# Five gather places instead of three, 336 dense tokens instead of 342, and a gate table in eight stages

## What is computed

```python
        q = (xb @ w_query).reshape(TOKEN_BLOCK, PEER_HEADS, 2, PEER_QDIM // 2)
        s = jnp.einsum("nhpd,hpkd->nhpk", q, sub_keys).astype(jnp.float32)
        sv, si = lax.top_k(s, PEER_TOPK)
        ...
        g = jax.nn.softmax(top_s, axis=-1).reshape(TOKEN_BLOCK, PEER_HEADS * PEER_TOPK)
        u = u_tab[eidx]
        hid = jax.nn.gelu(jnp.einsum("nd,ned->ne", xb, u), approximate=False)
        w = (g * hid.astype(jnp.float32)).astype(xb.dtype)
        return jnp.einsum("ne,ned->nd", w, v_tab[eidx])
```

## Time and profile before

| | |
|---|---|
| median of three runs | 3299.02 us (3294.02 to 3302.07) |
| the profiled execution's own time | 3297.2 us |
| its span, first to last instruction | 3295.1 us |
| TensorE busy | 3225.9 us (98%) |
| VectorE busy | 2697.7 us (82%) |
| ScalarE, GpSimd busy | 1053.1 us (32%), 1154.9 us (35%) |
| DMA, mean over the span | 278 GB/s, 914.55 MB |
| gathers | 171 of u, 171 of v |

### The profile page before, as it was taken

One profiled execution on the slowest core, in us unless ns is written; L12 is line 12 of the kernel. 1 busy time (PEld: TensorE's weight loads), 2 busy tenths in 40 slices (PEclk: granted clock), 3 DMA queues, 4 the chain that ended last, 5 costly groups with the idle time before them and its releaser, 6 DMA issues. The chain is left out here.

```text
span 3295.1 us, 48421 instructions
## 1 busy us (share of the span) xinstructions
PE 3225.9 (98%) x19393; PEld 2975.4 (90%) x19393; DVE 2697.7 (82%) x3810; ACT 1053.1 (32%) x1401; POOL 1154.9 (35%) x602
## 2 busy tenths in 40 slices
PE   6999999998999999999999999999999999999998
PEld 3788888888995448999999999999999999999998
DVE  2599999998885669968788888888688888888888
ACT  3223232323222004952323322323322323323332
POOL 2343333332541765013233333334133333233332
PEclk9999999999999999999999999999999999999999
DMA  9745454445557112569899999999799998999887
GB/s 400 282 165 172 157 175 161 167 169 214 196 184 288 64 39 98 226 261 362 337 371 359 355 358 362 353 346 367 291 360 356 357 351 346 361 351 353 341 341 306
DMA packets 174476, 914.55 MB, mean 278 GB/s; under 512 B 16303, under 2 KB 54104, under 8 KB 80088
## 3 DMA queue, kind: packets, MB, share of 16 engines
q1 hardware_dynamic: 125046, 553.37, 45.5%
q0 software_dynamic: 49248, 358.63, 28.0%
HBM read 876.31 MB, written 34.55 MB: 276 GB/s over the span
## 5 line engine op out<-in xcount | busy, mean ns | idle before, releaser
L1441 ACT ACTIVATE sb_raw_hi<-sb_raw_ring 128x2048 fp32r<-128x2048 f32 x256 | 491.0, 1918 | 1144.5 <-DMA sb_raw_ring<-in_v_t 561.3
L1962 DVE TENSOR_TENSOR sb_raw_lo<-sb_raw_ring,sb_raw_hi 128x2048 fp32r<-128x2048 f32 x256 | 585.0, 2285 | 107.1 <-ACT sb_raw_hi L1441 107.0
L1102 PE MATMUL ps_all<-sb_w_hi,sb_raw_hi 128*128 128x342 f32 x2032 | 639.5, 319 | 7.5 <-ACT sb_raw_hi L1441 3.9
L1041 PE MATMUL ps_all<-sb_h_hi,sb_raw_hi 128*128 128x342 f32 x2048 | 646.0, 320 | 0.0
L1041 PE MATMUL ps_all<-sb_h_lo,sb_raw_hi 128*128 128x342 f32 x2048 | 645.6, 320 | 0.0
L1103 PE MATMUL ps_all<-sb_w_lo,sb_raw_hi 128*128 128x342 f32 x2032 | 638.6, 320 | 0.0
L2291 POOL DMA_INDIRECT sb_gather_ring<-in_u_tab,sb_kept x171 | 293.3, 1715 | 747.4 <-DVE sb_kept L2092 571.0
L2291 POOL DMA_INDIRECT sb_gather_ring<-in_v_tab,sb_kept x171 | 298.7, 1747 | 625.6 <-DVE sb_acc_a L2105 425.4
L2195 POOL TENSOR_TENSOR sb_w_low<-sb_w_raw,sb_w_high 128x1536 fp32r<-128x1536 f32 (+1 forms) x63 | 260.0, 4127 | 406.8 <-ACT sb_w_high L1250 406.8
L1102 PEld LDWEIGHTS ps_all<-sb_w_hi,sb_raw_hi 128*128 128x128 f32 x2032 | 384.7, 189 | 10.0 <-ACT sb_raw_hi L1441 5.6
L1041 PEld LDWEIGHTS ps_all<-sb_h_lo,sb_raw_hi 128*128 128x128 f32 x2048 | 386.0, 188 | 0.0
(11 more groups left out here) (311 smaller groups left out, 5367.5 us busy)
## 6 DMA issues: line engine op xcount, KB each, us to landing
sb_raw_ring<-in_u_t SPq DMA_DIRECT2D x128, 1024.0 KB, 7.3
sb_raw_ring<-in_v_t SPq DMA_DIRECT2D x128, 1024.0 KB, 7.7
sb_arena<-in_ada_wt SPq DMA_DIRECT2D x96, 512.0 KB, 4.3
sb_w_raw<-in_w_t SPq DMA_DIRECT2D x32, 1024.0 KB, 5.8
...
```

What stands on the lines that cost most here:

```text
L1041: last = mm(acc, raw_hi[:, r[0], kk * P:(kk + 1) * P], part[:, kk, :], start=i == 0, stop=False)
L1102: mm(accs[c], v, w_hi[:, slots[e], :], start=e == 0, stop=False)
L1441: acti(raw_hi[:, k % 2, :], raw_ring[:, k % RAW, :], ACT.Copy).then_inc(S["un_hi"], 1)
L1962: vec.tensor_tensor(raw_lo[:, k % RAW, :], raw_ring[:, k % RAW, :], raw_hi[:, k % 2, :].bitcast(f32), ALU.subtract)\
```

## The change

XT goes from 42 to 48, so that ND = 336; the last tile's sparse tokens stand twice in the partitions (XG = 2, 96 of 128 rows used) and need 64 slots instead of 43. DOTS is 192, and there are 384 gathers instead of 342, spread over the same steps. The gate table has eight stages of 42 tokens. The ring has five places: while dots are taken, `acc_a` and `acc_x` (not yet accumulators) are places 3 and 4, and while v is accumulated, the two operands of the dots, `h2a` and `h2x`, are. `gather_places` gives each gather the allowed place that was used longest ago, and with it the gather whose use must be over; the first ten and the last six use three places only. The first two gathers into the new places also wait for `w_lo`, since the early units' results lie there. The load of the first two `last_x` tiles, which goes to `h2a` and `h2x`, moves from unit 137 to unit 251. To free two semaphores, `rows_in`, `dist_in` and `silu_in` become one, `head_in`, waited for at its full count by all.

```diff
-XT = 42
+XT = 48
...
+WIDE = 5
...
-STAGE = 38
+STAGE = 42
...
+def gather_places():
+
+    places, last = [], [-1] * WIDE
+    for n in range(2 * DOTS):
+        if n == DOTS:
+            last[GRING:] = [DOTS - 1] * (WIDE - GRING)
+        allowed = range(WIDE if 10 <= n < 2 * DOTS - 6 else GRING)
+        place = min(allowed, key=lambda p: last[p])
+        places.append((place, last[place]))
+        last[place] = n
+    return places
+
+
+GPLACES = gather_places()
+
+
+def gather_use(n):
+    return sum(p == GPLACES[n][0] for p, _ in GPLACES[:n + 1])
...
 def slot_at(n):
-    m, j = n // 4, n % 4
-    return (False, SLOTS + m) if j == 1 else (True, 3 * m + max(j - 1, 0))
+    m, j = n // 3, n % 3
+    return (False, SLOTS + m) if j == 1 else (True, 2 * m + j // 2)
...
-        stage = [placed(f"stage{n}", a, [P, NKEYS, STAGE]) for n, a in enumerate((M0, at))]
+        stage = [placed(f"stage{n}", a, [P, NKEYS, STAGE]) for n, a in enumerate((M0, at) if NSTAGE % 2 else (at, M0))]
...
+        def gather_at(n):
+            place = GPLACES[n][0]
+            if place < GRING:
+                return gather_ring[:, place, :]
+            return ((acc_a, acc_x) if n < DOTS else (h2a, h2x))[place - GRING]
...
-            sp.wait_ge(S["silu_in"], 32)
+            sp.wait_ge(S["head_in"], 96)
...
-                if k == TURN + 3:
-
-                    sp.wait_ge(S["gr_used"], DOTS)
+                if k == UNITS - 5:
+
+                    sp.wait_ge(S["gr_used"], 2 * DOTS - 6)
                     for t in range(2):
                         sp.dma_start(last_x[t], x1_d[t * P:(t + 1) * P, :]).then_inc(S["last_in"], 16)
...
-            dve.wait_ge(S["rows_in"], 48)
+            dve.wait_ge(S["head_in"], 96)
             e, z, q = lg_t
...
-                wait(dve, f"gr_in{n % GRING}", 16 * (n // GRING + 1))
-                ring = gather_ring[rows, n % GRING, :]
+                wait(dve, f"gr_in{GPLACES[n][0]}", 16 * gather_use(n))
+                ring = gather_at(n)[rows, :]
...
-                wait(pool, "gr_used", n - GRING + 1)
-                pool.indirect_dma_start(out=gather_ring[:, n % GRING, :], out_offset=None, in_=u_tab if n < DOTS else v_tab,
+                wait(pool, "gr_used", GPLACES[n][1] + 1)
+                if n < DOTS and GPLACES[n] in ((GRING, -1), (GRING + 1, -1)):
+                    pool.wait_ge(S["w_lo"], EARLY)
+                pool.indirect_dma_start(out=gather_at(n), out_offset=None, in_=u_tab if n < DOTS else v_tab,
```

More of the change, by code:

```diff
@@ L269, in build_program @@
         hid_all = take(DOTS)
+        at = max(at, SM + 2 * PEER_HEADS * NKEYS)
         raw_hi = rounded("raw_hi", at, [P, 2, D])
@@ L351, in bank @@
             return psum[:, i * NB:(i + 1) * NB]
-        names = """consts rows_in dist_in x_in sumsq silu_e silu colsT cols_ev lg_e
-            silu_rows silu_out silu_in col_in0 col_in1 col_in2 col_in3 col_a col_used late_cols late_t late_row late_out bias_in silu_w gate2_cols gate2_t gate2_bias gate2_row gate2_out
+        names = """consts head_in x_in sumsq silu_e silu colsT cols_ev lg_e
+            silu_rows silu_out col_in0 col_in1 col_in2 col_in3 col_a col_used late_cols late_t late_row late_out bias_in silu_w gate2_cols gate2_t gate2_bias gate2_row gate2_out
             ada_in0 ada_in1 ada_in2 ada_in3 ada_in4 ada_done ada_ev row_t mod_b xtr h_tmp h_high h_low
@@ L361, in build_program @@
             x1_out h2x_in xe_in un_in0 un_in1 un_in2 un_hi un_lo un_half un_done g_in0 g_in1 gelu gated w_hi w_lo y_ev
-            gr_in0 gr_in1 gr_in2 gr_used hid_gelu hid_w fin_in last_in last_rest y_last pick_x yt_done sq_done zs y y_out
+            gr_in0 gr_in1 gr_in2 gr_in3 gr_in4 gr_used hid_gelu hid_w fin_in last_in last_rest y_last pick_x yt_done sq_done zs y y_out
             dve pool spare""".split()
@@ L481, in _ @@
             piece_load(0, 3)
-            sp.dma_start(lg_all, decay.partition_broadcast(P)).then_inc(S["rows_in"], 16)
-            sp.dma_start(lam_in, lams.partition_broadcast(P)).then_inc(S["rows_in"], 16)
-            sp.dma_start(iota[:, :], iota_c).then_inc(S["rows_in"], 16)
+            sp.dma_start(lg_all, decay.partition_broadcast(P)).then_inc(S["head_in"], 16)
+            sp.dma_start(lam_in, lams.partition_broadcast(P)).then_inc(S["head_in"], 16)
+            sp.dma_start(iota[:, :], iota_c).then_inc(S["head_in"], 16)
             sp.wait_ge(S["silu_out"], 16)
             sp.wait_ge(S["ada_done"], ADA_PIECES)
-            sp.dma_start(dist, dist_c).then_inc(S["dist_in"], 16)
+            sp.dma_start(dist, dist_c).then_inc(S["head_in"], 16)
             for g in range(GROUPS):
@@ L497, in _ @@
             for g in range(GROUPS):
-                sp.dma_start(silu_b[:, g, :], silu_d[g:g + 1, :].partition_broadcast(P)).then_inc(S["silu_in"], 16)
-            sp.wait_ge(S["silu_in"], 32)
+                sp.dma_start(silu_b[:, g, :], silu_d[g:g + 1, :].partition_broadcast(P)).then_inc(S["head_in"], 16)
+            sp.wait_ge(S["head_in"], 96)
             head_loads(0, first=True)
@@ L1817, in plain @@
                 link(ins)
-            dve.wait_ge(S["dist_in"], 16)
+            dve.wait_ge(S["head_in"], 96)
             head_step(0, None, plain)
@@ L2097, in accumulate @@
                 rows = slice(0, P if own else XP)
-                wait(dve, f"gr_in{n % GRING}", 16 * (n // GRING + 1))
-                ring, acc = gather_ring[rows, n % GRING, :], (acc_a if own else acc_x)[rows, :]
+                wait(dve, f"gr_in{GPLACES[n][0]}", 16 * gather_use(n))
+                ring, acc = gather_at(n)[rows, :], (acc_a if own else acc_x)[rows, :]
                 if n - DOTS in (0, 1):
@@ L2263, in _ @@
                 x1_root(t)
-            pool.wait_ge(S["rows_in"], 48)
+            pool.wait_ge(S["head_in"], 96)
             for hd in range(PEER_HEADS):
```

2 lines of the change are left out of this document (1 added, 1 removed).

## The result

The changed kernel takes 3340.12 us (median of five runs, 3317.94 to 3348.89) against 3299.02 for the kernel before (3294.02 to 3304.53): a ratio of 1.0117, 95% interval 1.0077 to 1.0156. It is slower by some 39 us; the forecast was 3288 and the range ended at 3325. The profiled execution of the changed kernel took 3317.94 us and is the fastest of its five, so its trace shows only about half of the loss; the times of the other four lie 20 to 31 us above it.

A forecast was written before the change was run, and what follows sets the result against it. TensorE was taken to bound the expert loop, with DMA and VectorE close behind. Terms -28.8 - 2.3 + 11 + 6 + 3 = -11.1 us on 3297.2 gave 3286.1, forecast as a 3288 us median; range 3270 to 3325.

The forecast's parts named there:

- columns: Dense expert loop, units 16 to 255: 6 fewer columns at 0.41 ns each shorten every matmul; -28.8 us with two early units.
- gate table: Routing stage: 88 groups instead of 90, with narrower products on VectorE and TensorE; -2.3 us.
- before unit 25: First gathers into the new places wait for w_lo, so dots 10 and 11 run late and TensorE stops; +11 us.
- body: table loads, VectorE: Expert loop: more gathers make table loads land later, +6 us; VectorE at 90% stays below TensorE, 0.
- tail: Last units: residual tiles moved to unit 251, unit 255's load and VectorE's added accumulation, 1 us each; +3 us.
- head, and stops before 1500 us: Head: VectorE's decay work waits for all of head_in, silu broadcasts too, but an existing gap covers it; 0.
- The five places keep the gathers from being the limit: Gather ring in the loop: three places allow 3.8 us a gather plus the wait for POOL, against a pace of 4.5.
- Rival A: Expert loop: gathers saturate the DMA engines at 375 GB/s, so the loop loses 30 us; 3341 us, chance 0.17.
- Rival C: Expert loop: table loads land 2 us later instead of 1, losing 15 to 20 us; 3299 us, chance 0.25.
- 358 GB/s between HBM and SBUF: Quoted DMA limit per core: two units would take 16.0 us and the kernel some 3427 us; prediction sided with the trace.

The follow-up runs named there:

- run 3: Changed kernel with the new gather places first used from gather 14 instead of 10: 3328.76 us, 1.0095 of the kernel before.
- run 8: Changed kernel set back to the old sizes (342 dense tokens, 342 gathers), five places, new ones from gather 14: 3305.54 us, 1.0008 of the kernel before.
- run 4: Changed kernel with three gather places instead of five: 3414.46 us, 1.0346 of the kernel before.
- run 5: Changed kernel with VectorE's dots and accumulations over half the columns, all gathered bytes kept: 3304.31 us, 1.0006 of the kernel before.
- Run 11: Changed kernel with four gather places (fourth from gather 14) and a fourth raw place for table loads: 3290.12 us, 0.9969 of the kernel before.
- run 6: Changed kernel with 120 of the last tile's gathers fetching 4 KB rows instead of 8, VectorE's work kept: 3291.06 us, 0.9977 of the kernel before.
- run 9: Changed kernel with both halvings, VectorE's gather work and the last tile's gathered bytes: 3271.18 us, 0.9908 of the kernel before.

## Why the prediction was wrong

The prediction's terms against the two traces of the changed kernel, each less the trace of before, stops and half clock together (us):

| term | forecast | at 3317.94 | at 3333.72 |
|---|---|---|---|
| columns | -28.8 | -38 | -38 |
| gate table | -2.3 | -2.5 | -2.5 |
| before unit 25 | +11 | +11.5 | +11.9 |
| body: table loads, VectorE | +6 | +30 | +45 |
| tail | +3 | +15.6 | +15.4 |
| head, and stops before 1500 us | 0 | +3.4 | +4.0 |
| sum | -11.1 | +20 | +36 |
| measured, to the trace of before | | +20.7 | +36.5 |

- **Columns (-28.8): right in kind, too small.** A unit without a stop takes 7.38 us (forecast 7.40 to 7.42), where it took 7.54: 0.16 us in 240 units is 38. So between 342 and 336 a column is worth some 0.55 ns of a matmul; the 0.41 ns came from the step between 342 and 512. **Gate table (-2.3): right.** From unit 0 to unit 15 it is 200.2 us instead of 202.8.
- **Head waits (0): not settled.** Unit 0 starts at 1246.3 us in the one trace of before and at 1246.6 to 1249.6 in the thirteen with the merged wait; no run singled it out.
- **Stop before unit 25 (+11): right,** in cause and size. 9.70 us, and 5.6 us of work at a granted 0.50 behind it; run 3 takes away 13 of 41 us by the medians, run 8 takes 6 of 11.
- **"The five places keep the gathers from being the limit": right** (run 4).
- **Body ("I take +6"): this step failed.** It was 30 and 45 us in the two traces, in three parts. First, the table loads. The prediction had the place: "The loads behind a gate reload are those without slack". It priced them by all loads landing 1 us later. The median did: from issue to the high part, where that waited, 7.8 us became 9.0 and 8.8, and behind a reload 10.0 became 10.4 and 11.0. But the longest went from 14.0 to 17.3 and 21.8 us, against a slack of 12.9, and the longest are what stop TensorE: 14.2 and 25.6 us. I had priced the slack as landings that come 1 or 3 us later, and named about 30 us for the second; it was the right scale with too small a chance. Behind it was the choice of 422 GB/s over 15 us as the nearer figure and not 375 over 30. Second, VectorE: "It stays below TensorE, and its other work is not needed before 1.6 units later, so 0 as a bound." At the first down unit of each block its low part is needed at once, and TensorE waited 8.8 and 11.2 us for it; run 5 takes this away (0.9). Third, the half clock behind these stops, which was counted at unit 25 alone, cost another 8.6 and 10.7 us.
- **Rival A was near in time (3341) by luck, and half right in mechanism.** It had the engines saturated at 375. Runs 5 and 11 moved 380 and 384 with all bytes. What ran out was the time between issue and need: with three raw places the next load is not issued until TensorE has let go of the place, so lost time turns into a lower rate, and the lower rate looks like a limit. Rival C had the mechanism of the table loads' part and about its size (15 to 20 us), and its sign, idles of TensorE after gate reloads, came true for some of them; it ended at 3299 because it had VectorE, the tail and the half clock as the forecast did.
- **Tail (+3): too small.** At unit 251 the charge was 1 us and the stop 3.7; for VectorE's last accumulations it was 1 us, and the stops are 6.4 and 1.5 us, since the last gathers are late too.
- The rule that the prediction quoted from the Trainium skill (*DMA: Bandwidth & Descriptors*, *Where 436 GB/s comes from*), 358 GB/s between HBM and SBUF, is not borne out by the runs either: 371 to 384 GB/s over 700 us and more.

The loss of the changed kernel, in short, on the trace at 3333.72 us: 40 us won; 12 given back before unit 25, 15 in the tail, 4 before them, 45 in the loop.

**Open:** No run moved or split the gate reloads, so that it is they that make the next load late is read from the traces alone. That bursts of gathers add to it (D) is not shown: in the 17 to 24 us before each of those stops 4 or 5 gathers went out, little more than the mean of one in 4.5 us. Why halving the bytes also frees VectorE's results (run 6) was not followed up. Run 11 still lies 19 us above run 9; its trace shows 12.4 us of waits for VectorE's results, and its own runs spread over 25 us where those of the kernel before spread over 10. Which instructions of VectorE hold POOL up was not separated either.
